# The even layer's 31-tap depthwise convolution computed on TensorE instead of VectorE and GpSimd, with two score banks in the attention beside it

## The chip, the cores and the metric

The kernel runs on one core of one Trainium2 chip. The metric is the device time of one execution in microseconds (us); everything is float32. Engines are called PE (TensorE), DVE (VectorE), ACT (ScalarE), POOL (GpSimd) and SP (SyncE, which only issues transfers).

## The reference, cut to what matters

The program chains three networks over 256 tokens of width 1024. The change lies in the second one, in its even layer. There, one half of the layer is an attention of 8 heads over 512 keys (256 context keys and 256 own keys), and the other half is a gated convolution over the tokens:

```
glu  = a * sigmoid(b)                       # 512 channels, from one projection of the normed tokens
conv = sum over tap 0..30 of  w[tap, channel] * glu[token + tap - 15, channel]  + bias[channel]
y    = silu(layer_norm(conv) * g + b)       # mean and variance over the 512 channels of a token
x    = x + gate * (concat(attention, y) @ w_out)
```

Each channel is convolved by itself (depthwise). The layer is followed by a router and a mixture of 16 experts with 12 MB of weights each, the first of two such mixtures.

## The kernel before

Everything is written out by hand: each engine runs its own function (`even_pe`, `even_act`, `even_dve`, `even_pool`), whose order in the code is the engine's order, and engines wait for one another by named marks (`pe_s`, `act_s`, `dve_s`, `pool_s`). `claim` makes PE wait until a PSUM bank has been read out.

**Weights.** SP loads weight chunks of 2 MB in the order in which they are used, each into the next of 6 slots of `ring`. A chunk is loaded as soon as PE has used the chunk that stood 6 before it in that slot. Around the change the order is: the layer's projections with pieces of the conditioning matrix (`ada1_0` to `ada1_5`), then `ada1_6` to `ada1_11`, `ev_out0`, `ev_out1`, `memkv0`, and three parts (g1, u0, d0) of the first expert. So `ev_out0` waits for the use of `ada1_6`, and d0 for the use of `ada1_11`. The part g0 of the first expert goes into `spare` and `p_buf` after the last transposition of the attention (`b2.T15`), the next ones wait for the use of `ev_out0` and `ev_out1`, and u1 and d1 for the router's logits.

**The attention `b2`.** 16 units (a head's 128 queries by 512 keys) run through a software pipeline of 19 steps. In step i, PE computes the scores of units i and i+1 if i is even (L713), transposes the exponentials of unit i-2 (L738) and multiplies those of unit i-3 with the values (L747). DVE takes a unit's row minimum, ACT the exponential, the copy of the transposed exponentials and the output. The list `scores` names the banks for scores: with `THREE = (4, 3, 2)` the scores of unit i wait for the exponential of unit i-3, with `TWO = (4, 2)` for that of unit i-2.

**Beside the attention**, after each step, a hook `also` runs on each engine. On PE (`beside_b2`) it multiplies with one piece of the conditioning matrix in each of steps 0 to 5 (`ada_rows_pe`, 8 matmuls of a 128x32 stationary tile by 512 columns, one after another for the four column groups of the array, L950), turns the result into columns in step 8 (L962, L965), and does the layer norm's sums with matmuls in steps `LN_AT` = 9, 12 and 15 (L1410, L1416, L1422).

**The convolution.** Channels lie on partitions, four tiles of 128, tokens along the row, with 15 zeros on either side in `glu`. DVE does tile 1 before the attention and tiles 2 and 3 partly before it and partly in its hook in steps 0 to 8 (`conv31`, one instruction per tap and tile, L1487); POOL does tile 0 (`conv31_pool`, two instructions per tap, L1645 and L1647). The PE sum of step 9 waits for both.

Of the kernel before, what the change touches and what calls it, by code (L numbers as in the profile page):

```python
# [22 lines left out]
S = 256  # L23
# [61 lines left out]
def onehots():  # L85
# [11 lines left out]
    for i in range(512):  # L97
# [8 lines left out]
        ("mem_norm_3", 16), ("ev_conv_w_2", 124), ("ev_conv_b_2", 4), ("ev_ln_g_2", 4), ("ev_ln_b_2", 4),  # L106
# [22 lines left out]
def expert_order(a):  # L129

    return a.reshape(-1, 2, P, 4).transpose(0, 1, 3, 2).reshape(-1, P)


def columns(name, a):

    a = np.asarray(a)
    if name == "norm2_g_2":
        return expert_order(a)
    if name == "ada_b_2":
        b = a.reshape(2, 6, D)  # L140
        return np.concatenate([expert_order(b[l, v]) if v in (3, 4) else b[l, v].reshape(-1, P) for l in range(2) for v in range(6)])
    return a.reshape(-1, P)
# [145 lines left out]
def program(nc, A, out, planned):  # L288
# [12 lines left out]
    with ctx:  # L301
# [1017 lines left out]
        glu = view(10752, 4, S + 30)  # L1319
        cv = view(11896, 4, S)  # L1320
        catT = view(12920, 8, S)
# [51 lines left out]
        ADA_COLUMNS = 8  # L1373
        TAPS_FIRST, TAPS_BEFORE = 5, 8

        def even_pe():
# [19 lines left out]
            def beside_b2(step):  # L1396
                if step < 12 - ADA_FIRST:
                    ada_rows_pe(12 + ADA_FIRST + step)
                elif step == ADA_COLUMNS:
                    ada_columns_pe(1)  # L1400
                layer_norm_sums(step)

            def layer_norm_sums(step):


                if step == LN_AT:
                    claim(LN_BANK)
                    waits(t_, (pool_s, "conv0"), (dve_s, "conv3"))
                    for k in range(4):
                        ins = t_.matmul(bank[LN_BANK][:, 0:S], ones128, cv[:, k, :], start=(k == 0), stop=(k == 3))  # L1410
                    ins.then_inc(*pe_s.signals("ln0"))
                elif step == LN_AT + 3:
                    waits(t_, (act_s, "cv sq"))
                    for t in range(2):
                        for k in range(4):
                            ins = t_.matmul(bank[LN_BANK][:, t:t + 1], cv_sq[:, k, P * t:P * t + P], constant("one"), start=(k == 0), stop=(k == 3),  # L1416
                                            skip_group_check=True)
                    ins.then_inc(*pe_s.signals("ln1"))
                elif step == LN_AT + 6:
                    waits(t_, (pool_s, "ln.rstd"))  # L1420
                    for t in range(2):
                        ins = t_.matmul(bank[LN_BANK][:, P * t:P * t + P], stats[:, 64 + t:65 + t].to_broadcast([P, P]), ident, start=True, stop=True,  # L1422
                                        skip_group_check=True)
                    ins.then_inc(*pe_s.signals("ln2"))

            attention_pe("b2", units2, before=turned("kx", kx_items) + turned("qx", qx_items), also=beside_b2)
# [6 lines left out]
        def even_act():  # L1433
# [7 lines left out]
            for t in range(2):  # L1441
                a.activation(view(12920, 2, D)[:, t, :], mem_raw[0][:, t, :], ACT.Square, accum_out=stats[:, 104 + t:105 + t])\
                    .then_inc(*act_s.signals(*(["nmem.ss"] if t else [])))
            for i in range(2):
                a.wait_ge(*pe_s.after(f"ev_glu{i}.acc1"))
                a.activation(pT_buf[:, i, :], bank[acc_banks(f"ev_glu{i}") + 1][:, :], ACT.Sigmoid).then_inc(*act_s.signals(f"ev_glu{i}.free1"))
            for t in range(2):
# [16 lines left out]
            attention_act("b2", units2, before=[(dve_s, "glu1")], also=beside_b2)  # L1464
# [6 lines left out]
        LN_AT = 9  # L1471
        LN_BANK = 5
        TAPS_AT = [TAPS_BEFORE + n for n in (0, 3, 6, 9, 12, 15, 18, 20, 22, 23)]

        def conv31(taps, tiles):

            v = nc.vector
            for tap in taps:
                for k in tiles:
                    w = col("ev_conv_w_2", 4 * tap + k)  # L1480
                    src = glu[:, k, tap:tap + S]
                    if tap == taps[0]:
                        v.wait_ge(*dve_s.latest())
                    else:
                        v.wait_ge(dve_s.sem, dve_s.n - (len(tiles) - 1))
                    if tap:
                        ins = v.scalar_tensor_tensor(out=cv[:, k, :], in0=src, scalar=w, in1=cv[:, k, :], op0=ALU.mult, op1=ALU.add)  # L1487
                    else:
                        ins = v.tensor_scalar(cv[:, k, :], src, w, col("ev_conv_b_2", k), ALU.mult, ALU.add)
                    ins.then_inc(*dve_s.signals(*([f"conv{k}"] if tap == CONF_K - 1 else [])))  # L1490
# [57 lines left out]
        def even_dve():  # L1548
# [14 lines left out]
            for i in range(2):  # L1563
# [4 lines left out]
                if i == 0:  # L1568
                    conv31(range(CONF_K), [1])
            conv31(range(TAPS_FIRST), [2, 3])  # L1570
            rope_raw_dve(0)
            conv31(range(TAPS_FIRST, TAPS_BEFORE), [2, 3])
# [8 lines left out]
            def conv_and_norm(step):  # L1581
                if step == ADA_COLUMNS + 1:
                    ada_columns_dve(1)
                if step < LN_AT:
                    conv31(range(TAPS_AT[step], TAPS_AT[step + 1]), [2, 3])
                elif step == LN_AT + 1:
                    v.wait_ge(*pe_s.after("ln0"))
                    v.tensor_scalar(mean, bank[LN_BANK][:, 0:S], 1.0 / 512, None, ALU.mult).then_inc(*dve_s.signals("ln0"))
                    v.wait_ge(*pool_s.after("conv0"))
# [5 lines left out]
                elif step == LN_AT + 3:  # L1595
# [5 lines left out]
            attention_dve("b2", units2, also=conv_and_norm)  # L1601
# [5 lines left out]
        def context_pool():  # L1607

            waits(nc.gpsimd, (pe_s, "ada.e0"), (dve_s, "y.e3"), (dve_s, "branch_a0.free1"))
# [8 lines left out]
        def even_pool():  # L1618
# [6 lines left out]
            g.wait_ge(*dve_s.after("glu0"))  # L1625
            g.wait_ge(*pe_s.after("hx.T3"))
            conv31_pool(range(0, 15))
            for t in range(2):
                rstd_pool("ev_q_g", *[b[:, 8 * t:8 * t + 8] for b in q_ss], HD, tile=t)
                if t == 0:  # L1630
                    conv31_pool(range(15, 18))
            conv31_pool(range(18, CONF_K))
            head_norm_pool("ln", 1, width=512)

        def conv31_pool(taps):

            g = nc.gpsimd
            tmp = [flat_xn[:, 1024 + 256 * i:1280 + 256 * i] for i in range(2)]
            for tap in taps:
                w = col("ev_conv_w_2", 4 * tap)  # L1640
                src = glu[:, 0, tap:tap + S]
                if tap:
                    if tap >= 3:
                        g.wait_ge(pool_s.sem, pool_s.n - 1)
                    g.tensor_scalar(tmp[tap % 2], src, w, None, ALU.mult).then_inc(*pool_s.signals())  # L1645
                    g.wait_ge(*pool_s.latest())
                    g.tensor_tensor(cv[:, 0, :], cv[:, 0, :], tmp[tap % 2], ALU.add)\  # L1647
                        .then_inc(*pool_s.signals(*(["conv0"] if tap == CONF_K - 1 else [])))
                else:
                    g.tensor_scalar(cv[:, 0, :], src, w, col("ev_conv_b_2", 0), ALU.mult, ALU.add).then_inc(*pool_s.signals())  # L1650

# [1414 lines left out]
```

## Time and profile before

| | us |
|---|---|
| median of 3 runs | 2328.44 (2328.24 to 2328.85) |
| the profiled execution | 2325.14 |
| its span in the trace | 2322.9 |
| PE busy | 1960.7 (84%) |
| DVE busy | 594.2 (26%) |
| ACT busy | 290.4 (13%) |
| POOL busy | 131.7 (6%) |
| chain that ended last: PE, DMA, DVE | 64%, 32%, 2% |

Busy shares are averages over stages with different limits, so the stage that is changed has to be read from the trace by itself. Times in the trace count from the span's start. The attention `b2` runs from 416 to 476 us, the first mixture of experts from about 536 us.

### The profile page before, as it was taken

Reading aid. Unit: us, or ns where it says so; the run is one execution under the profiler, and the core shown is the slowest. Engines: PE = TensorE matmul, PEld = TensorE weight load, DVE = VectorE, ACT = ScalarE, POOL = GpSimd, SP = SyncE. Lnnn points to the kernel's source line nnn. Section 1 sums busy time; section 2 is a strip of 40 time slices with the busy share of each in tenths; the row PEclk is TensorE's granted clock in tenths of the full one; section 3 lists DMA queues with packets and bytes.
Section 4 is the critical chain, followed back from the end, with each engine's and each line's share of the span. In section 5 each row is a group of like instructions: output and inputs, shape, how many; then the busy total and the mean of one; then the engine's idle time right before and its main releaser. Section 6 shows DMA issues by size and latency. Waiting matters only on the chain.

```text
span 2322.9 us, 30376 instructions
## 1 busy us (share of the span) xinstructions
PE 1960.7 (84%) x12649; PEld 1153.0 (50%) x12649; DVE 594.2 (26%) x1686; ACT 290.4 (13%) x750; POOL 131.7 (6%) x177
## 2 busy tenths in 40 slices
PE   8999999899655566699966556669999999999999
PEld 4455556555322222387532223224568854548874
DVE  1323337712000000122210000004625411334430
ACT  1023411431000000010200000001500001300000
POOL 0200006400000000000000000002100000010000
PEclk9999999899888887899997887879999999999999
DMA  9658347839999999975899999999234444324420
GB/s 365 250 187 318 128 163 256 324 116 382 425 426 427 427 426 427 388 228 217 333 425 426 426 427 425 427 422 336 73 110 145 155 147 151 109 73 146 163 107 18
DMA packets 191439, 634.48 MB, mean 273 GB/s; under 512 B 6529, under 2 KB 90641, under 8 KB 158840
## 3 DMA queue, kind: packets, MB, share of 16 engines
q1 hardware_dynamic: 186912, 623.79, 69.2%
q0 software_dynamic: 1504, 5.83, 0.7%
q10 hardware_dynamic: 2936, 3.66, 0.4%
q8 instruction: 61, 1.00, 0.2%
q14 instruction: 26, 0.21, 0.0%
HBM read 632.15 MB, written 1.09 MB: 273 GB/s over the span
## 4 chain that ended last, share of the span: by engine, by line
PE 64%; DMA 32%; DVE 2%; ACT 1%; issue 1%; POOL 0%; SPq 0%; DVEq 0%; ACTq 0%
DMA ring<-in_moe_w_down 32%; PE bank L647 17%; PE bank L662 17%; PE bank L2573 7%; PE bank L2050 4%; PE bank L999 3%; PE bank L747 2%; PE bank L713 1%; PE bank L950 1%; PE bank L738 1%; PE bank L2225 1%; PE bank L2034 1%; PE bank L1952 1%; PE bank L2529 1%; DVE arena L1487 1%; PE bank L561 1%
## 5 line engine op out<-in xcount | busy, mean ns | idle before, releaser
L2034 PE MATMUL bank<-ring,arena 128*32 128x256 f32 x3968 | 303.0, 461 | 185.9 <-DMA ring<-in_moe_w_up 113.2
L2034 PEld LDWEIGHTS bank<-ring,arena 128*32 128x32 f32 x3968 | 138.8, 128 | 336.6 <-DMA ring<-in_moe_w_up 147.3
L647 PE MATMUL bank<-ring,hT 128*128 128x512 f32 (+2 forms) x704 | 299.1, 583 | 5.0 <-DVE hT L2213 2.9
L662 PE MATMUL bank<-xn,ring 128*128 128x256 f32 x1280 | 276.6, 379 | 0.0
L662 PEld LDWEIGHTS bank<-xn,ring 128*128 128x128 f32 x1280 | 243.2, 190 | 33.0
L2050 PE MATMUL bank<-ring,arena 128*32 128x256 f32 x1984 | 162.7, 485 | 76.9 <-DMA ring<-in_moe_w_down 66.9
L647 PEld LDWEIGHTS bank<-ring,hT 128*128 128x128 f32 x704 | 133.6, 192 | 157.3 <-issue 153.8
L2573 PE MATMUL bank<-ring,arena 128*128 128x512 f32 x352 | 151.6, 592 | 0.0
L2050 PEld LDWEIGHTS bank<-ring,arena 128*32 128x32 f32 x1984 | 73.2, 134 | 154.5 <-DMA ring<-in_moe_w_down 83.4
L1843 DVE TENSOR_TENSOR arena<-arena,bank 128x256 f32<-128x256 f32 x32 | 13.5, 421 | 495.2 <-ACT arena L1904 495.2
L662 PE MATMUL bank<-hT,ring 128*128 128x256 f32 x512 | 111.3, 379 | 1.3 <-ACT arena L1357 1.3
L1904 ACT ACTIVATE arena<-bank 128x256 f32<-128x256 f32 x32 | 12.3, 383 | 769.6 <-PE bank L2034 769.6
L2573 PEld LDWEIGHTS bank<-ring,arena 128*128 128x128 f32 x352 | 66.8, 190 | 82.8 <-issue 82.3
L662 PEld LDWEIGHTS bank<-hT,ring 128*128 128x128 f32 x512 | 97.0, 190 | 15.4 <-issue 2.3
L1846 DVE TENSOR_TENSOR arena<-bank,arena 128x256 f32<-128x256 f32 x32 | 13.6, 424 | 249.4 <-PE bank L2050 249.4
L2623 DVE SCALAR_TENSOR_TENSOR arena<-arena,cols 128x256 f32<-128x256 f32 x176 | 71.5, 477 | 0.0
L2611 DVE TENSOR_TENSOR arena<-bank,arena 128x512 f32<-128x512 f32 x44 | 30.4, 691 | 152.6 <-PE bank L662 140.9
L999 PE MATMUL bank<-ring,hT 128*128 128x512 f32 x128 | 69.0, 631 | 0.4 <-ACT arena L1009 0.4
L510 POOL TENSOR_SCALAR stats<-stats 128x1 f32<-128x1 f32 (+7 forms) x34 | 7.6, 223 | 1082.8 <-DVE stats L410 450.6
L647 PE MATMUL bank<-ring,arena 128*128 128x512 f32 (+1 forms) x160 | 64.8, 562 | 2.9 <-ACT arena L579 2.9
L747 PE MATMUL bank<-arena,pT_buf 128*128 128x64 f32 (+1 forms) x408 | 62.6, 278 | 0.6 <-ACT pT_buf L770 0.3
L747 PEld LDWEIGHTS bank<-arena,pT_buf 128*128 128x128 f32 x408 | 56.8, 201 | 6.9 <-ACT pT_buf L770 2.6
(409 smaller groups left out, 1837.8 us busy)
## 6 DMA issues: line engine op xcount, KB each, us to landing
ring<-in_moe_w_gate SPq DMA_DIRECT2D x62, 2048.0 KB, 26.5
ring<-in_moe_w_up SPq DMA_DIRECT2D x62, 2048.0 KB, 26.0
ring<-in_moe_w_down SPq DMA_DIRECT2D x62, 2048.0 KB, 26.1
ring<-in_ada_w SPq DMA_DIRECT2D x24, 2048.0 KB, 11.7
ring<-in_w_up SPq DMA_DIRECT2D x44, 1024.0 KB, 7.6
ring<-in_w_in SPq DMA_DIRECT2D x11, 2048.0 KB, 17.5
ring<-in_w_down SPq DMA_DIRECT2D x10, 2048.0 KB, 7.8
ring<-in_w_out SPq DMA_DIRECT2D x6, 2048.0 KB, 22.3
```

The source lines that it names most:

```text
L561: ins = nc.tensor.transpose(bank[b][0:n, at:at + tokens], src(t), constant("ident", tokens)[:, 0:tokens])
L647: ins = t_.matmul(bank[b][:, 0:n], lhsT(k)[:, P * t:P * t + P], w[:, k, c0:c0 + n], start=(k == 0), stop=(k == kt - 1))
L662: ins = t_.matmul(bank[b][:, 256 * (j % 2):256 * (j % 2) + 256], w[:, k, P * j:P * j + P], rhs[:, k, :], start=(k == 0), stop=(k == 7), sk ...
L713: t_.matmul(score_bank(i, scores)[:, 0:u["keys"]], u["q"], u["k"], start=True, stop=True)\
L738: ins = t_.transpose(bank[6 + j % 2][0:n, P * k:P * k + P], p[:, P * k:P * k + n], ident)
L747: ins = t_.matmul(bank[j % 2][:, 0:v.shape[-1]], pT_buf[0:n, j % 2, P * k:P * k + P], v, start=(k == 0), stop=(k == len(u["v"]) - 1))
L999: ins = t_.matmul(bank[GM_BANK][:, :], hT[:, k, P * t:P * t + P], slot(name)[:, k, :], start=(k == 0), stop=(k == 7))
L2034: ins = t_.matmul(bank[4][32 * j:32 * j + 32, at:at + 256], xs_now[b][:, 4 * (c % 2) + k, :], w(k)[:, 256 * j:256 * j + 256], start=(c % 2 ...
L2050: ins = t_.matmul(bank[6][32 * j:32 * j + 32, 0:256], hidT[b][:, f % 2, 32 * (f // 2):32 * (f // 2) + 32], w(k)[:, 256 * j:256 * j + 256], ...
L2573: ins = t_.matmul(bank[b][:, :], actT[:, f, P * t:P * t + P], w[:, k, 512 * half:512 * half + 512], start=(f == 0), stop=(f == FF_TILES - 1))
L2611: v.tensor_tensor(up_buf[i % 2][:, 2 * t:2 * t + 2, 2:2 + S], bank[acc_banks(name) + t][:, :].rearrange("p (k s) -> p k s", s=S), by_token ...
L2623: ins = v.scalar_tensor_tensor(out=dst, in0=src, scalar=w, in1=dst, op0=ALU.mult, op1=ALU.add)
```

## The change

Each channel tile k is now convolved by 32 matmuls on PE. The 128 channels are taken in four quarters q of 32. For each quarter, the 128 partitions of a matmul's input hold the quarter's 32 channels four times, and copy j is shifted by j tokens (`shifted[k]`). The stationary tile (128x32) is four diagonal blocks with the weights of taps 4g to 4g+3, so that one matmul adds four taps; 8 groups g cover 32 taps (the last has weight zero). The four quarters write the four column groups of one bank. The parts:

- POOL builds the stationary tiles by multiplying the constant `fold` with the tap weights (`tap_weights_pool`): tiles 0 to 2 early, before its load of the context, into `spare`, tile 3 after the hx turn into `xn`.
- The shifted copies are transfers from SBUF to SBUF: 16 of them for tiles 0 and 1 together, issued by ACT between the two sigmoids of the gate, and 16 each for tiles 2 and 3, issued by POOL after the norm of the queries (`shift_pool`).
- PE runs the matmuls in halves of 16 in steps 0, 1, 2, 3, 5, 6, 7 and 8 of `b2` (`conv31_pe`). Four of the six conditioning pieces move from steps 0 to 5 to steps 9 to 13: they now stand in steps 4, 9, 10, 11, 12, 13. The columns move from step 8 to 16, the layer norm's sums from 9, 12, 15 to 10, 13, 16 and to bank 3.
- DVE only adds the bias while copying two tiles out of the bank, in steps 4 and 9 (`conv31_dve`). All its taps and those of POOL are gone.
- The attention uses `TWO` score banks, since bank 3 holds the convolution.

```diff
-        ADA_COLUMNS = 8
-        TAPS_FIRST, TAPS_BEFORE = 5, 8
+        ADA_BESIDE = (4, 9, 10, 11, 12, 13)
+        ADA_COLUMNS = 16
+        CONV_AT = {0: (0, 0), 1: (0, 1), 2: (1, 0), 3: (1, 1), 5: (2, 0), 6: (2, 1), 7: (3, 0), 8: (3, 1)}
...
+            def conv31_pe(k, half):
+                if half == 0:
+                    if k % 2 == 0:
+                        claim(CONV_BANK)
+                    t_.wait_ge(s_shift[max(0, k - 1)], 16 * 16)
+                    waits(t_, (pool_s, f"tap weights{k}"))
+                for g in range(4 * half, 4 * half + 4):
+                    for q in range(4):
+                        ins = t_.matmul(bank[CONV_BANK][32 * q:32 * q + 32, S * (k % 2):S * (k % 2) + S], tap_w[k][:, q, g, :],
+                                        shifted[k][:, q, 4 * g:4 * g + S], start=(g == 0), stop=(g == 7), skip_group_check=True)
...
-            attention_pe("b2", units2, before=turned("kx", kx_items) + turned("qx", qx_items), also=beside_b2)
+            attention_pe("b2", units2, before=turned("kx", kx_items) + turned("qx", qx_items), also=beside_b2, scores=TWO)
...
+                if i == 0:
+                    waits(a, (act_s, "nmem.ss"), (dve_s, "glu0"))
+                    for j, q in itertools.product(range(4), range(4)):
+                        a.dma_start(shifted01[32 * j:32 * j + 32, :, q, 0:SHIFTED], glu[32 * q:32 * q + 32, 0:2, j:j + SHIFTED]).then_inc(s_shift[0], 16)
...
-        LN_AT = 9
-        LN_BANK = 5
+        LN_AT = 10
+        LN_BANK = CONV_BANK
...
-                if i == 0:
-                    conv31(range(CONF_K), [1])
-            conv31(range(TAPS_FIRST), [2, 3])
...
+                if step in (4, 9):
+                    conv31_dve(step == 9)
...
+            tap_weights_pool(range(3))
...
+            tap_weights_pool([3])
...
-            conv31_pool(range(18, CONF_K))
+            waits(g, (dve_s, "glu1"), (pe_s, "ev_q.acc1"))
+            shift_pool(2)
+            waits(g, (pe_s, "hm0.T3"))
+            shift_pool(3)
```

PE, the first steps of `b2` before (L713 scores, L738 transpositions, L747 values, L950 conditioning):

```order
L713 MATMUL bank<-arena 128x512 x2
L950 MATMUL bank<-ring,arena 32x512 x16
L713 MATMUL bank<-arena 128x512 x2
L738 MATMUL bank<-const,p_buf 128x128 x4
L950 MATMUL bank<-ring,arena 32x512 x8
L738 MATMUL bank<-const,p_buf 128x128 x4
L747 MATMUL bank<-arena,pT_buf 128x64 x4
L950 MATMUL bank<-ring,arena 32x512 x8
```

One conditioning piece (8 matmuls) stands in each step, two of them together in the second row.

The same place in the changed kernel, where the lines are L716, L741, L750 and L953, and L1441 is the convolution:

```order
L716 MATMUL bank<-arena 128x512 x2
L1441 MATMUL bank<-arena,spare 32x256 x32
L716 MATMUL bank<-arena 128x512 x2
L741 MATMUL bank<-const,p_buf 128x128 x4
L1441 MATMUL bank<-arena,spare 32x256 x16
L741 MATMUL bank<-const,p_buf 128x128 x4
L750 MATMUL bank<-arena,pT_buf 128x64 x4
L1441 MATMUL bank<-arena,spare 32x256 x16
L716 MATMUL bank<-arena 128x512 x2
L741 MATMUL bank<-const,s_buf 128x128 x4
L750 MATMUL bank<-arena,pT_buf 128x64 x4
L953 MATMUL bank<-ring,arena 32x512 x8
```

The convolution stands where the conditioning stood, and only one conditioning piece is left among the first nine steps.

PE in the changed kernel from step 12 to the end of step 16 (L953 conditioning, L1421 the sums of squares, L965 and L968 the columns, L1427 the last matmuls of the layer norm; the repeated column rows are cut off):

```order
L953 MATMUL bank<-ring,arena 32x512 x8
L1421 MATMUL bank<-const,xn 128x1 x8
L716 MATMUL bank<-arena 128x512 x2
L741 MATMUL bank<-const,p_buf 128x128 x4
L750 MATMUL bank<-arena,pT_buf 128x64 x4
L741 MATMUL bank<-const,p_buf 128x128 x4
L750 MATMUL bank<-arena,pT_buf 128x64 x4
L741 MATMUL bank<-const,s_buf 128x128 x4
L750 MATMUL bank<-arena,pT_buf 128x64 x4
L965 MATMUL bank<-const,arena 128x24
L968 MATMUL bank<-const,arena 64x8 x2
```

Before, these columns stood in step 8; now they stand two steps from the end.

POOL in the changed kernel, from the norm of the memory tokens to the layer norm:

```order
L1662 TENSOR_TENSOR xn<-const,cols 128x256 x4
L513 TENSOR_SCALAR stats<-stats 128x8
L516 TENSOR_TENSOR stats<-stats,const 128x8
L513 TENSOR_SCALAR stats<-stats 128x8
L516 TENSOR_TENSOR stats<-stats,const 128x8
L1670 DMA hT<-arena 32x284 x16
L1670 DMA arena<-arena 32x284 x16
L513 TENSOR_SCALAR stats<-stats 128x2
L516 TENSOR_TENSOR stats<-stats,const 128x2
```

Between the queries' norm and the layer norm, where POOL had its taps 18 to 30, it now issues 32 transfers.

## Rows read from the trace of the kernel before

**Rows 1.** Chain that ended last: start us, us, what; 329 to 620 us.
```profile
369.46 3.57 PE bank L950 x32
...
414.09 1.08 PE bank L561 x8
...
416.26 1.15 PE bank L713 x4
...
458.05 0.59 PE bank L738 x4
458.64 0.84 PE bank L747 x8
...
463.24 1.81 PE bank L1416 x16
...
474.00 1.80 PE bank L747 x16
...
535.96 7.09 PE bank L2034 x128
...
563.44 26.17 DMA ring<-in_moe_w_down
```

**Rows 2.** Windows: start:end, length, busy (instructions) of PE, PEld, DVE, ACT, POOL; granted clock, DMA share, GB/s.
```profile
416.26:475.80 59.54, 55.87 (x372) 37.68 (x372) 39.35 (x89) 25.36 (x65) 19.98 (x25) 0.86 0.67 257
420.00:440.00 20.00, 18.03 (x140) 8.58 (x132) 19.64 (x39) 6.25 (x17) 14.35 (x16) 1.00 1.06 393
440.00:445.00 5.00, 3.32 (x16) 1.92 (x16) 4.93 (x13) 2.65 (x8) 0.00 (x0) 0.75 1.03 440
445.00:450.00 5.00, 5.00 (x28) 4.40 (x26) 4.13 (x11) 2.63 (x7) 0.00 (x0) 0.50 0.96 401
465.00:470.00 5.00, 5.00 (x27) 3.43 (x26) 1.58 (x5) 1.99 (x6) 2.06 (x4) 0.66 0.04 13
475.80:480.20 4.40, 1.10 (x8) 0.87 (x9) 0.76 (x2) 4.20 (x8) 0.00 (x0) 0.98 0.90 363
```

**Rows 3.** Groups of PE instructions, 416.2 to 475.9 us: count, busy us, mean ns, idle before.
```profile
L713 PE MATMUL bank<-arena 64*128 64x512 f32 x32 | 10.9, 761 | 4.1 <-ACT p_buf L779 2.6 <-DVE arena L587 1.1 <-ACT s_buf L779 0.4
```

**Rows 4.** The same view of DVE, 365 to 480 us.
```profile
L1487 DVE SCALAR_TENSOR_TENSOR arena<-arena,cols 128x256 f32<-128x256 f32 x90 | 52.2, 614 | 1.8
```

**Rows 5.** Timeline of ACT: start us, us, engine, line, operation [idle before].
```profile
1.72 0.64 ACTq L1051 DMA_DIRECT2D p_buf<-in_onehots  x1
...
31.38 0.34 ACTq L1070 DMA_DIRECT2D bias_rows<-s_buf  x1
...
387.07 0.60 ACT L1446 ACTIVATE pT_buf<-bank 128x512 f32<-128x512 f32 x1 [16.98 <-PE bank L662]
```

**Rows 6.** Timeline of POOL.
```profile
283.76 0.91 POOL L1610 DMA_DIRECT2D arena<-in_ctx  x1 [166.84 <-DVE arena L1194]
...
372.85 0.83 POOL L1647 TENSOR_TENSOR arena<-arena,xn 128x256 f32<-128x256 f32 x1
...
408.83 1.84 POOL L513 TENSOR_TENSOR stats<-stats,const 128x8 f32<-128x8 f32 x1
...
1592.39 0.54 POOL L2682 DMA_DIRECT2D small<-in_gla_gate_w  x1
...
1687.49 0.99 POOL L2689 DMA_DIRECT2D arena<-in_w_in_gla  x1 [2.11 <-DVE arena L2666]
```

**Rows 7.** Transfers, 395 to 480 us: target, queue, count, KB each, median us to landing.
```profile
small<-in_moe_w_r POOLq DMA_DIRECT2D x1, 64.0 KB, 2.2
```

**Rows 8.** Timeline of SP's transfers.
```profile
435.88 0.38 SPq L2956 DMA_DIRECT2D ring<-in_moe_w_down  x1
...
474.03 0.33 SPq L2938 DMA_DIRECT2D spare<-in_moe_w_gate  x1
```

## What the change should do

> **What bounds the kernel now.** I read the chain that ended last first, between 329 and 620 us. It runs over PE up to 563 us and from there over the expert weights [rows 1]. From 563 us the mixture is paced by the transfers, and how early their stream starts is set by PE: part g0 is issued at 474.03, after the attention's last transposition, and later parts wait for the output projection and the router. So what `b2` gains or loses should arrive at the end unchanged, as long as the weights before it land in time.
>
> Then I cut out `b2`, from its first scores at 416.26 to the end of the last product at 474.00 + 1.80 = 475.80, as one window [rows 1, 2]. Its length is 59.54 us, PE is busy for 55.87, at a mean granted clock of 0.86. The reader should see two regimes. From 420 to 440 DVE is busy for 19.64 of 20 us while PE has gaps; the gaps before scores are 4.1 us in all, mostly for ACT, which itself is behind DVE's taps [rows 2, 3]. After that DVE falls idle and PE is busy all the time, but at a clock of 0.75 and then 0.50 (the lower level, 1.2 instead of 2.4 GHz). So DVE bounds the first third, and PE the rest.
>
> **What PE has to do.** A mean clock of 0.86 says that 0.14 x 59.54 = 8.3 us of the window were lost to the lower level. PE's own work at full clock is then 55.87 - 8.3 = 47.6 us; the other 3.7 us are gaps. 47.6 + 8.3 + 3.7 = 59.6 closes.
>
> **The change part by part.**
>
> *Removed.* 90 of DVE's tap instructions in the trace, 52.2 us busy [rows 4], and all of POOL's. Those before 416 us are worth nothing: PE goes from work to work, and `b2` starts when the queries are turned (414.09 and 1.08 us, then their copy), which comes after ACT's copies, not after taps [rows 1]. Those within `b2` are worth at most the 3.7 us of gaps, plus what the lower clock costs after those gaps.
>
> *Added on PE.* 4 tiles x 32 = 128 matmuls of a 128x32 stationary tile by 256 columns over four column groups. The first expert's gate and up products have just this form: 128 records, that is 64 matmuls, in 7.09 us at full clock [rows 1]. So the convolution costs 2 x 7.09 = 14.2 us. I see no price below this; the conditioning's form gives the same rate (16 matmuls of 512 columns in 3.57 us, 0.22 each, half of it per 256 columns), and it stands between pieces of the attention already.
>
> PE then has 47.6 + 14.2 = 61.8 us of work at full clock. That is above today's 59.5 us even before any gap. The work removed from DVE bought at most 12 us (3.7 gaps + 8.3 clock), and the convolution costs more than that.
>
> *Moved on PE.* Conditioning pieces, columns and layer norm cost the same wherever they stand, except by the clock. The sums of squares are 16 records of one column in 1.81 us [rows 1], and after them the clock was 0.66 in the window from 465 to 470, some 3.4 us at the lower level, a cost of 1.7 us [rows 2]. They now stand in step 13, behind a conditioning piece, which is denser. The columns (8 and 24 wide) move to step 16, two steps from the end, after two steps that hold attention alone. I take one such stretch of low clock in the changed kernel, 1.7 us; the bounds are none (0) and both with the tail of the attention (3.4).
>
> *Two score banks.* The scores of an even step now wait for the exponential of the unit just before, which ACT finishes in the odd step ahead. After its transposition in that step PE still has a product (0.84 us) and, in steps 1 to 13, a piece of convolution or conditioning (1.8 us each: half of 3.57) [rows 1]; ACT needs a copy and an exponential over 512 columns, which at the 0.60 us of its gate over 512 columns [rows 5] are some 1.3 us. So PE comes later than ACT. Only in steps 14 to 16, where ACT also copies the conditioning sums out, do I count 0.3 us. Bounds: 0, and the same 4.1 us that scores wait today [rows 3].
>
> *DVE* has two biased copies of 128x512 in place of the taps, about 0.7 us each, behind which the next row minimum waits; PE is not waiting for DVE by then. I count nothing.
>
> *ACT* issues 16 transfers after the first gate. Its issues take 0.34 to 0.64 us, 5 to 10 us in all, and it waits 16.98 us for PE there [rows 5]. Hidden; they land 25 us before they are needed.
>
> *POOL, tap weights.* 12 operations of 128x256 early, at some 0.83 us each 10 us, in an idle time of 166.84 us ahead of the context's load [rows 6]; the 4 for tile 3 take 3.3 us in POOL's idle time before the taps of today. Hidden.
>
> *POOL, shifts.* This is the part that can hurt. POOL is done with the queries' norm at 408.83 + 1.84 = 410.7, a little earlier without taps, and then issues 32 transfers one after another. Its issues take 0.54 to 0.99 us; the shortest is the one with the fewest rows (16), the longest the one with the most (1024 short runs) [rows 6]. These have 32 rows, so I take 0.6: tile 2 is issued by 420.3, tile 3 by 429.9, and landed 2.2 us later [rows 7]. PE needs tile 2 in step 5 and tile 3 in step 7. Step 7 comes after four pairs of scores (1.1 each), six transpositions and five products (0.59 or less, and 0.84), six half tiles and one conditioning piece (1.8 each): about 24 us after 416.3, at 440. There are 8 us to spare. With 0.99 each the last lands at 444.6, 4 to 5 us late.
>
> The Trainium skill (DMA: Bandwidth & Descriptors, "Anatomy of one DMA") gives a transfer issued by GpSimd about 2.0 us of fixed cost from setup to completion; the 2.2 us of the trace agree, and the rule changes nothing so long as issues follow each other without waiting for landings.
>
> *SP.* With the conditioning pieces used later, `ev_out1` to d0 are issued in steps 9 to 13 instead of 1 to 5 (the last at 435.88 today [rows 8]). In the new order, with step 7 at 440 and some 4 us a step, that is 448 to 464 us. Five chunks of 2.1 MB at some 400 GB/s [rows 2] take 26 us, so d0 lands near 473, and g0 is behind it as today. The output projection needs `ev_out1` only 15 us later, and the experts start at 536. Nothing is late. The cover is some 20 us for the projection and 60 for d0.
>
> **Sum.** 61.8 (work) + 1.7 (clock) + 0.3 (banks) = 63.8 us. The mean clock is rounded, by up to 0.3 us in this sum; I take 63.6, against 59.5: +4.1 us. The profiled execution would go from 2325.1 to 2329.2, and the median of the runs, 3.3 us above it, from 2328.44 to 2332.5. A difference of 0.2% (4.66 us) is about what a measurement of this kernel can tell from no change, so this lies just inside "no change", at 0.18%.
>
> **A rule weighed.** In the trace PE is busy for 5.00 of 5.00 us at a clock of 0.50 between 445 and 450, so being busy alone doesn't bring the clock back; what ended it was the layer norm's sums over 256 columns. The Trainium skill (TensorE: Matmul & The Clock Gate, "What's actually happening") says that the gate opens with how busy PE has recently been. Taken plainly, a stage without gaps would then hold 2.4 GHz throughout. By the trace I lose 1.7 us, by the rule nothing; the rule is the second case below.
>
> **The rivals.**
>
> 1. *The forecast*, one stretch of low clock and no late copy: 2332.5. Chance 0.45.
> 2. *Full clock throughout*: 61.8 + 0.3, +2.5 us: 2330.9. For it: no gaps are left. Against it: one-column matmuls and columns remain. Chance 0.17.
> 3. *The shifts come late*, the case on the slower side. POOL's issues serialize behind something, each taking 0.99 us or more. From 0.86 us on (32 x 0.86 + 2.2 + 410.7 = 440.4) step 7 waits, and each further 0.1 us costs 3.2 us. At 1.1 us it waits 7.7 us, and a gap of that size brings the clock down for another 1.7: +4.1 + 9.4 = 13.5 us, 2341.9. At 0.99, with the clock, it is about 2338. Against it: the rows of 0.54 and 0.64. Chance 0.17.
> 4. *PE falls behind its own sum*: two banks leave gaps as wide as today's (3.7 us) and both low-clock stretches come (another 1.7): +9.5, 2337.9. Chance 0.13.
> 5. *Faster*: this needs the attention's transpositions and products to shrink when a dense piece stands before them. The 32 pieces (a transposition of 0.59 us or a product of 0.84 each [rows 1]) would have to lose 0.2 us each, since 61.8 must fall below 54.8. Weight loads are busy 37.68 of 59.54 us, so something can hide, but in steps with conditioning today the transposition is not shorter. At the decision point 2323.7. Chance 0.08.
>
> **The numbers.** Slower by over 0.2%: rivals 3 and 4, 0.30, and 0.12 of the forecast's own spread, which ends at the boundary: 0.42. Faster: 0.08. Same: 0.50. The range goes from 2328.0 (full clock, some weight loads hidden) to 2341.0 (late shifts).
>
> **What would show it.** In the window of `b2`: a length near 63.6 us, PE busy in nearly all of it, the convolution at 14.2 us and a clock of 0.94 to 1.00; DVE busy for less than 20 us of it. Before step 7 no wait for a transfer. g0 is issued 4 us later than 474.03, and the mixture starts and ends 4 us later. I am wrong if the convolution's matmuls take other than 0.11 us each, if a wait of PE for the shift stands in step 5 or 7, if the clock stays low with PE full, or if the mixture's stream doesn't move with the end of `b2`.

## The result

| | before | changed |
|---|---|---|
| median, us (lowest to highest), 12 runs each | 2326.99 (2323.29 to 2331.93) | 2333.78 (2329.03 to 2342.36) |
| ratio, 95% interval | | 1.0034 [1.0024, 1.0044] |
| profiled execution, span, us | 2325.14, 2322.9 | 2329.93, 2328.1 |
| `b2`, first scores to end of the last product, us | 59.54 | 65.24 |

The changed kernel is slower by 0.34%, 5.6 to 10.2 us by the interval; the medians differ by 6.8 us. The forecast was +4.1 us or 0.18%, just inside the 0.2% that it took for "no change". The measured difference lies beyond that, in a case to which it gave 0.42. The sign and the place were right, the size was too small.

The changed kernel's page, engines' busy time in us and share:

```profile
PE 1966.6 (84%) x12905; PEld 1155.3 (50%) x12905; DVE 546.8 (23%) x1595; ACT 290.1 (12%) x750; POOL 100.9 (4%) x164
```

The changed kernel's chain that ended last (start us, us, what), around `b2`:

```profile
413.63 0.77 DVE arena L590 x2
414.39 0.30 issue
414.69 1.13 PE bank L716 x4
415.82 3.59 PE bank L1441 x64
...
420.47 0.59 PE bank L741 x4
421.06 1.86 PE bank L1441 x32
...
453.46 1.92 PE bank L1415 x8
455.38 0.44 PE bank L741 x4
...
466.13 1.88 PE bank L1421 x16
...
473.49 0.34 PE bank L968 x4
473.83 0.33 PE bank L965 x2
...
476.92 3.02 PE bank L750 x16
...
484.36 22.33 PE bank L650 x48
...
567.49 26.28 DMA ring<-in_moe_w_down
```

From 414.69 us on the chain runs over PE alone: no tap and no row minimum of DVE is left on it. The output projection starts at 484.36 instead of 480.22, and the mixture's piece of the chain, the transfer of 26 us, at 567.49 instead of 563.44 [rows 1]. What `b2` gained arrived at the end.

Windows of the changed kernel (columns as in [rows 2]): `b2` as a whole, then cut where the clock falls.

```profile
414.69:479.94 65.25, 65.24 (x628) 41.61 (x628) 16.35 (x45) 24.74 (x65) 10.37 (x22) 0.98 0.79 282
414.69:477.20 62.51, 62.51 (x617) 39.07 (x617) 15.06 (x37) 24.07 (x64) 10.15 (x22) 1.00 0.79 282
477.20:479.94 2.74, 2.73 (x14) 2.54 (x12) 1.28 (x9) 0.67 (x2) 0.22 (x1) 0.50 0.88 278
```

PE is busy for 65.24 of 65.25 us. For 62.5 us it has the full clock, and the last 2.74 us run at the lower level. Against [rows 2] the stage lost its 3.7 us of gaps and most of its low clock, and gained more PE work than that.

The groups of PE in the changed kernel, 414.6 to 485 us, columns as in [rows 3]:

```profile
L716 PE MATMUL bank<-arena 64*128 64x512 f32 x32 | 9.0, 640 | 1.1 <-DVE arena L590 1.1
```

The scores wait once, for the queries' copy before the first of them. The waits for ACT of [rows 3] are gone, in spite of two banks.

Timeline of POOL in the changed kernel, the norm of the queries and its 32 transfers:

```profile
405.59 1.69 POOL L516 TENSOR_TENSOR stats<-stats,const 128x8 f32<-128x8 f32 x1
407.23 7.96 POOL L1670 DMA_DIRECT2D hT<-arena  x16
415.18 7.83 POOL L1670 DMA_DIRECT2D arena<-arena  x16
```

The last issue ends at 423.0, and these transfers land 5.6 to 5.9 us (median) after their issue. Step 7 needs them at 439.6 and finds them there.

### The profile page after: what moved, and what is told of

It reads as the page before. It is cut to its first block, busy times and chain, and to the rows that moved or that the text cites. A ratio compares the mean times of both kernels' runs of the same rounds, so it can differ in the third digit from the quotient of the medians.

```text
span 2328.1 us, 30805 instructions
## 1 busy us (share of the span) xinstructions
PE 1966.6 (84%) x12905; PEld 1155.3 (50%) x12905; DVE 546.8 (23%) x1595; ACT 290.1 (12%) x750; POOL 100.9 (4%) x164
## 4 chain that ended last, share of the span: by engine, by line
PE 65%; DMA 32%; DVE 1%; ACT 1%; issue 1%; POOL 0%; SPq 0%; DVEq 0%; ACTq 0%
DMA ring<-in_moe_w_down 32%; PE bank L665 17%; PE bank L650 17%; PE bank L2590 6%; PE bank L2067 4%; PE bank L1002 3%; PE bank L750 2%; PE bank L953 2%; PE bank L716 2%; PE bank L741 1%; PE bank L2242 1%; PE bank L2051 1%; PE bank L1969 1%; PE bank L2546 1%; PE bank L564 1%; PE bank L1441 1%
## 5 line engine op out<-in xcount | busy, mean ns | idle before, releaser
L750 PE MATMUL bank<-arena,pT_buf 128*128 128x64 f32 (+1 forms) x408 | 62.9, 279 | 0.4 <-ACT pT_buf L773 0.3
L773 ACT ACTIVATE pT_buf<-bank 128x256 f32<-128x256 f32 (+3 forms) x120 | 43.6, 363 | 133.2 <-PE bank L741 133.0
L750 PEld LDWEIGHTS bank<-arena,pT_buf 128*128 128x128 f32 x408 | 56.8, 201 | 6.4 <-ACT p_buf L782 2.0
```

What stands on the lines that cost most here:

```text
L750: ins = t_.matmul(bank[j % 2][:, 0:v.shape[-1]], pT_buf[0:n, j % 2, P * k:P * k + P], v, start=(k == 0), stop=(k == len(u["v"]) - 1))
L773: a.activation(pT_buf[0:n, j % 2, 0:kt * P], bank[6 + j % 2][0:n, 0:kt * P], ACT.Copy)\
```

## The experiments

Three batches of kernels, each against the kernel before on its own chip (2328.43; 2326.58 over 23 runs; 2327.71 over 23 runs). "Stage" is `b2` as above. For a single run no ratio is given.

### What the convolution on PE costs

**A quarter of it** (changed kernel; groups 0 and 7 of the 8 alone, so 24 of the 32 taps are left out):

```diff
-                for g in range(4 * half, 4 * half + 4):
+                for g in ([7] if half else [0]):
```

> The changed kernel with 8 of the 32 convolution matmuls per tile (groups 0 and 7 of 8); the convolution is therefore incomplete, everything else is unchanged. Theory A (the attention stage is now nothing but PE's work, 65.25 us): 24 of 32 matmuls less are 11.1 us less work, so the stage from first scores to last product falls to 54 us plus whatever gaps open, 54 to 57 us, and the mixture starts 8 to 11 us earlier. Rival B (the transfers of the shifted copies or the two score banks hold the stage): the stage falls by under 4 us, with waits in place of the matmuls.

**Twice** (changed kernel; each matmul of the convolution is issued twice, so most taps count double):

```diff
-                for g in range(4 * half, 4 * half + 4):
+                for g in [g for g in range(4 * half, 4 * half + 4) for _ in range(2)]:
```

> The changed kernel with each convolution matmul issued twice (so the sums come out double where they accumulate). Theory A: 14.75 us more PE work, so the stage grows from 65.25 to 80 us and the whole by 14.75 us (profiled execution near 2344.7). Rival B (PE has hidden slack): less than 10 us.

The stage as a window, first with a quarter:

```profile
416.54:472.94 56.40, 55.75 (x436) 34.66 (x436) 16.56 (x45) 24.68 (x65) 9.65 (x20) 0.96 0.89 316
```

and with the double:

```profile
415.79:495.33 79.54, 79.53 (x884) 48.90 (x884) 16.36 (x45) 24.75 (x65) 9.50 (x20) 0.98 0.63 223
```

The double adds 14.3 us to the stage (79.54 - 65.24) and 16 us to the execution (2345.97 us). The quarter takes 8.8 us off; three quarters of 14.75 would be 11.1, but 0.65 us of gaps and a lower mean clock came back (0.96). Its execution took 2323.43 us. In both traces the clock is at its lower level at the first scores (2.10 and 2.08 us instead of 1.13), and it had fallen ahead of them, before the edited lines run; more on this under "The rest of the size". So the stage is PE's work and nothing that the convolution could hide behind: nearly every microsecond added is paid.

### Two banks and moved pieces, without the convolution

**Two banks alone** (kernel before; all three engines):

```diff
-            attention_pe("b2", units2, before=turned("kx", kx_items) + turned("qx", qx_items), also=beside_b2)
+            attention_pe("b2", units2, before=turned("kx", kx_items) + turned("qx", qx_items), also=beside_b2, scores=TWO)
```

> The kernel before with only the score banks cut from three to two. Theory A: DVE's taps bound the first half of the stage and PE waits there anyway, so the stage stays within 1 us of 59.54 us. Rival C (two banks are a cost of their own in the changed kernel): 3 us or more longer, with longer waits of the scores for the exponentials.

**Two banks and the pieces moved** as in the change, taps still on DVE and POOL:

```diff
-        ADA_COLUMNS = 8
+        ADA_BESIDE = (4, 9, 10, 11, 12, 13)
+        ADA_COLUMNS = 16
...
-        LN_AT = 9
-        LN_BANK = 5
+        LN_AT = 10
+        LN_BANK = 3
```

> The kernel before with two banks and with the conditioning pieces, columns and layer norm in the steps of the changed kernel, the taps still on DVE and POOL. Theory A: the first nine steps stay at DVE's pace with PE emptier (five conditioning pieces, 9.3 us, move behind them), so the stage grows by 6 to 9 us to 66 to 69 us, and the clock is low for longer. Rival D (the moved pieces cost nothing, only the convolution does): within 2 us of 59.54.

With two banks alone the stage takes 63.90 us, 4.4 more than before. The group of the scores there:

```profile
L713 PE MATMUL bank<-arena 64*128 64x512 f32 x32 | 10.9, 761 | 7.5 <-ACT p_buf L779 5.1 <-ACT s_buf L779 1.3 <-DVE arena L587 1.1
```

The wait for ACT's exponentials goes from 3.0 [rows 3] to 6.4 us; the forecast that the stage stays within a microsecond was wrong. Of the 4.4 us, 2.7 are gaps. The other 1.6 are pieces of PE at the lower clock, and not all of them come from the banks: in this trace, too, the clock was low at the first scores (2.10 instead of 1.15 us). With the pieces moved as well, the stage as a window:

```profile
418.84:491.75 72.91, 61.55 (x372) 42.83 (x372) 39.40 (x89) 25.54 (x65) 19.93 (x25) 0.75 0.58 216
```

13.4 us longer than before, also more than expected: 11.4 us of gaps, and a mean clock of 0.75. The execution took 2342.88 us. The same layout in the changed kernel has no gap. The layout is thus bad with empty steps and DVE's taps, and good with the convolution in the steps and the taps gone; this run does not say which of the two differences does it.

### An earlier place for the columns

Changed kernel, pieces in steps 4 to 9 and the columns in step 11, so that the columns are followed by more work:

```diff
-        ADA_BESIDE = (4, 9, 10, 11, 12, 13)
-        ADA_COLUMNS = 16
+        ADA_BESIDE = (4, 5, 6, 7, 8, 9)
+        ADA_COLUMNS = 11
...
-                elif step == ADA_COLUMNS + 2:
+                elif step == ADA_COLUMNS + 4:
```

> The changed kernel with the conditioning pieces in steps 4 to 9 and the columns in step 11 instead of 16. Theory A says that PE's work is the same, and that the columns and sums near the end brought the low clock from 477 to 487 us, worth 1.3 us in the stage and 1.5 us of the output projection: the stage falls from 65.25 to about 64 us if the low clock goes, and the kernel gains 1 to 3 us over the changed one, still slower than before by 2 to 5 us. Rival: the low clock only moves to step 13, and nothing is gained.

Measured: 2339.03 us (6 runs), 1.0052 [1.0037, 1.0066] of before, where a gain of 1 to 3 us over the changed kernel was expected. The interval overlaps with the changed kernel's, so that the timing alone does not tell the two apart; the stages do (72.29 us busy against 65.24). Windows of that kernel after the pieces are used up:

```profile
465.00:470.00 5.00, 5.00 (x27) 4.19 (x28) 1.78 (x8) 1.85 (x5) 0.00 (x0) 0.65 0.35 144
470.00:475.00 5.00, 5.00 (x25) 4.99 (x24) 0.00 (x0) 2.14 (x5) 0.00 (x0) 0.50 0.00 0
475.00:480.00 5.00, 5.00 (x20) 3.49 (x20) 1.97 (x9) 1.44 (x4) 1.66 (x3) 0.50 0.00 2
```

PE is busy for every microsecond, with attention, the layer norm's sums and columns, and the clock is at its lower level for about 20 us. In the changed kernel the conditioning pieces of steps 9 to 13 stand among this work, and the clock is 1.00 to 477.2 us. So the late place of pieces and columns, which the prediction costed as neutral but for one stretch of 1.7 us, was worth 7 us of stage (72.29 against 65.24), or 4 against the longer of the changed kernel's two traces (68.67, below).

### What the taps cost on DVE and POOL

Here a new theory was tested: that the removed work was slow only because DVE and POOL did it at the same time.

**All four tiles on DVE** (kernel before, three banks, POOL has no taps):

```diff
-        TAPS_FIRST, TAPS_BEFORE = 5, 8
+        TAPS_FIRST, TAPS_BEFORE = 4, 7
...
-                    conv31(range(CONF_K), [1])
+                    conv31(range(17), [0, 1])
+            conv31(range(17, CONF_K), [0, 1])
...
-            conv31_pool(range(0, 15))
...
```

All of POOL's taps are left out, and each step's share of DVE's taps is set anew.

> The kernel before with all four tiles' taps on DVE and none on POOL or PE. In the trace of before a tap takes 0.66 us while POOL works and about 0.45 us after it has stopped. Theory A (DVE's pace sets the first half of the attention stage, and POOL's taps slow DVE's): 124 taps at 0.47 us are 58 us, 33 us of room before the stage, 25 us in nine steps, so the stage is within 2 us of 59.5 us although DVE does a third more taps. Rival: a tap takes 0.6 us without POOL too, and the stage grows by 8 us or more.

**The same, measured again** beside the changed kernel:

> The same kernel as with all four tiles on DVE, timed again for a narrower interval: 0.996 to 0.998 of before, with an attention stage of 50 to 52 us.

> The changed kernel again, on the same chip as the run above. Theory A: the stage is PE's work and always 65 to 67 us whatever the low clock does elsewhere; the kernel is 0.3% slower than before, and 0.6% (14 us) slower than the one with all taps on DVE, which is what the two stages differ by (65.2 - 50.2 = 15).

**POOL's taps taken away** (kernel before; DVE's taps as they were; tile 0 is left out and filled with zeros):

```diff
-            conv31_pool(range(0, 15))
+            g.memset(cv[:, 0, :], 0.0).then_inc(*pool_s.signals("conv0"))
...
-                if t == 0:
-                    conv31_pool(range(15, 18))
-            conv31_pool(range(18, CONF_K))
```

> The kernel before without POOL's taps: tile 0 of the convolution is left out (filled with zeros), DVE has exactly the taps of before. Theory E (POOL's taps and DVE's taps slow each other, so that a DVE tap takes 0.61 us on average instead of 0.48): the steps 0 to 4 of the attention stage fall from some 4.2 us to PE's pace of 3.7, the gaps of PE and with them the low clock go, and the stage falls from 59.54 us to 50 to 52 us, as with all four tiles on DVE. Rival (the stage got short in that experiment for another reason): the tap stays near 0.6 us and the stage within 2 us of 59.5.

| kernel | median, us (runs) | ratio to before | stage, us | PE busy | clock |
|---|---|---|---|---|---|
| all on DVE | 2319.84 (10) | 0.9970 [0.9960, 0.9980] | 50.19 | 50.08 | 0.97 |
| all on DVE, again | 2321.44 (11) | 0.9983 [0.9973, 0.9993] | 50.23 | 50.13 | 0.97 |
| changed, again | 2335.65 (12) | 1.0033 [1.0021, 1.0045] | 68.67 | 68.66 | 0.92 |
| POOL's taps away | 2317.87 (1) | | 49.88 | 49.87 | 0.97 |

DVE's taps in the trace of the kernel before, within the stage (416 to 441 us), beside the row minimum, which reads from PSUM:

```profile
L1487 DVE SCALAR_TENSOR_TENSOR arena<-arena,cols 128x256 f32<-128x256 f32 x34 | 19.3, 619 | 0.4
L810 DVE TENSOR_REDUCE row_min<-bank 128x1 f32<-128x512 f32 x6 | 4.1, 681 | 1.4 <-PE bank L713 1.4
```

The same without POOL's taps:

```profile
L1487 DVE SCALAR_TENSOR_TENSOR arena<-arena,cols 128x256 f32<-128x256 f32 x36 | 15.3, 482 | 0.4
L810 DVE TENSOR_REDUCE row_min<-bank 128x1 f32<-128x512 f32 x7 | 4.8, 686 | 1.4 <-PE bank L713 1.4
```

Nothing was changed on DVE, yet a tap takes 482 instead of 619 ns; the row minimum takes the same. The 619 is itself a mean over two stretches. POOL's last tap operation ends at 435.0 us, and the trace of the kernel before, from 416 to 435 and from 436 to 447 us, has

```profile
L1487 DVE SCALAR_TENSOR_TENSOR arena<-arena,cols 128x256 f32<-128x256 f32 x24 | 15.0, 676 | 0.3
L1487 DVE SCALAR_TENSOR_TENSOR arena<-arena,cols 128x256 f32<-128x256 f32 x20 | 8.6, 481 | 0.3
```

So a tap costs 676 ns beside POOL and 481 once POOL is quiet, in one and the same execution. Six taps and a row minimum fill a pipeline step, so 0.8 us a step by the means and 1.2 us while POOL works, and without POOL's taps PE no longer falls behind. The Trainium skill (SBUF — State Buffer, "SBUF: two separate sides") says that VectorE and GpSimd share a pair of ports, which an operation of DVE with two SBUF inputs must have for itself against a GpSimd operation that reads SBUF. The trace agrees on which instruction is slowed: the tap, with two inputs in SBUF, is, and the row minimum, with one in PSUM, is not. That POOL's taps slow DVE's is shown by the run without them; that the ports are the way in which they do it is the page's account, and beyond this agreement no run here tests it.

With all 120 of its taps on DVE the group reads:

```profile
L1487 DVE SCALAR_TENSOR_TENSOR arena<-arena,cols 128x256 f32<-128x256 f32 x120 | 49.6, 481 | 0.8
```

DVE does 120 taps in less time (49.6 us) than 90 beside POOL (52.2 [rows 4]). POOL's taps, 60 operations in that stretch, were worth less than nothing. The second measurement, 0.9983, lies just above the 0.996 to 0.998 expected of it. The stage falls to 50.2 us, 15 us below the changed kernel's; it had been expected within 2 us of 59.5, so the theory was right on the tap and far too cautious on what it is worth. Of its 9.3 us against before, 2.3 to 2.7 were given back ahead of it: it starts at 418.93 and 418.57 instead of 416.26, in both traces with a mean clock of 0.91 between 200 and 240 us, where before has 0.96 and the changed kernel 1.00. The code of PE is the same there; I have no cause for it.

**All on DVE, but with two banks:**

> All four tiles on DVE, with two score banks instead of three. With three banks the stage took 50.19 us. Theory A: two banks cost only where the exponential of the unit just before is held up behind DVE's taps, and DVE is now nearly at PE's pace in the steps, so the scores of even steps wait a little: 51 to 54 us. Rival C (two banks cost 4 us wherever they stand): 54 us or more.

The stage takes 61.82 us instead of 50.19, with PE busy for 58.34 at a clock of 0.83: 3.5 us of gaps for ACT's exponentials and the rest low clock. The execution took 2326.64 us. My theory gave this at most 54 us and missed. But not all of the 11.6 us are the banks' price. The stage's first 5 us here, and with three banks:

```profile
415.87:421.00 5.13, 5.13 (x24) 1.34 (x28) 2.99 (x7) 0.78 (x2) 0.00 (x0) 0.58 1.05 388
418.93:424.00 5.07, 5.07 (x38) 1.54 (x40) 3.85 (x8) 0.78 (x2) 0.00 (x0) 1.00 1.06 388
```

The clock of 0.58 stands for some 2 us (0.42 x 5.13, an estimate), and it had fallen before the first scores, where the two kernels do not differ.

**One tile on PE in its gaps ahead of `b2`, three on DVE, three banks:**

```diff
-                    conv31(range(CONF_K), [1])
+                    conv31(range(CONF_K), [0])
...
+            conv31_pe(0)
             turn_pe("qx", qx_items, before=[(dve_s, "rope q")])
+            conv31_pe(1).then_inc(*pe_s.signals("conv1"))
```

> Tile 1 on PE, in the gaps before the attention where PE waits for ACT (half before and half behind the turn of the queries), tiles 0, 2 and 3 on DVE, none on POOL; three score banks and the pieces in the steps of before. Theory A: DVE's share inside the stage falls to 17 taps of two tiles (16 us in nine steps), below PE's pace, and PE has 49 to 50 us of work without the convolution: the stage starts 1 us later and takes 51 to 54 us, so the kernel is 4 to 7 us faster than before. Rival: the gaps before the stage don't hold the matmuls and DVE stays the pace: within 1 us of before.

PE's two halves of that tile in this kernel's chain:

```profile
414.80 1.86 PE bank L1409 x32
416.67 1.02 PE bank L564 x8
417.69 1.86 PE bank L1409 x32
```

Measured: 2322.59 us (12 runs), 0.9980 [0.9971, 0.9989]; stage 51.52 us. DVE's taps take 483 ns here too. It is better than before, because POOL's taps are gone, and no better than the kernel with nothing on PE: the gaps it fills cost about 1 us more ahead of the stage.

## Why the prediction was right or wrong

**What bounds the stage: right as far as it went.** PE at its own work with no gaps, and the shift passed on one to one (+4.14 us at the output projection, +4.05 at the mixture). The 4.14 are the stage's 5.70 less 1.57 by which the stage starts earlier. It starts earlier because before has a stretch of low clock near 221 us that this execution of the changed kernel lacks; PE's code is the same there. So it is luck that the later pieces moved by just the 4.1 us of the forecast, and that the profiled execution took 2329.93 us where 2329.2 was forecast.

**The term that was mis-sized most: "PE's own work at full clock is 47.6".** It subtracted 0.14 x 59.54 = 8.3 us as lost to the lower clock, as if every piece took twice as long there. The chain shows otherwise. Before, at the lower level:

```profile
443.44 2.08 PE bank L713 x4
445.52 1.04 PE bank L738 x4
446.57 1.60 PE bank L747 x8
...
448.87 0.55 PE bank L962 x2
449.42 0.34 PE bank L965 x4
...
454.19 2.80 PE bank L1410 x8
```

and the same pieces at full clock, where POOL's taps were away:

```profile
442.32 1.06 PE bank L713 x4
443.38 0.59 PE bank L738 x4
443.97 0.84 PE bank L747 x8
...
445.00 0.34 PE bank L965 x4
445.34 0.33 PE bank L962 x2
...
448.79 1.78 PE bank L1410 x8
```

Scores go from 2.08 to 1.06, but the columns' 8-wide matmuls take 0.34 at either level, the 24-wide 0.55 and 0.33, a transposition 1.04 and 0.59. Added up piece by piece over before's slow pieces, the low clock cost 7.0 us, not 8.3. Part of the difference are the 8-wide matmuls, and part is time in which the clock was low while PE had nothing to do, as before the scores at 443.44, and which costs nothing. PE's own work at full clock was thus 55.87 - 7.0 = 48.9 us, 1.3 more than the prediction had. In the changed kernel it still cost 1.3: the last 2.74 us at half clock, mostly the last product (3.02 instead of 1.80). The clock gave back 5.7 us where 8.3 - 1.7 = 6.6 were counted.

**The convolution: 14.75 us, not 14.2.** 3.59 + 6 x 1.86. The expert's products, from which the rate was read, take 7.09 us for 128 records, 1.77 for 32. Each of the six pieces that stand alone takes 0.09 more than that, and the two in a row at the start together 0.05 more.

**Gaps: right.** 3.7 us gone, and none came. (The 4.1 us of [rows 3] that served as a bound hold 1.1 us ahead of the first scores, outside the stage.)

**Two banks: right here, for a reason that was only half seen.** They open no gap in the changed kernel. In the two kernels of before's layout, with DVE's taps and steps of attention alone, the stage grew by 4.4 and 11.6 us, of which gaps are 2.7 and 3.4 and the rest is clock, not all of it theirs. The prediction covered them with 1.8 us of other work in each odd step. That this work is needed is not shown. With a quarter of the convolution each step has under 0.5 us of it, and the scores of that kernel read

```profile
L716 PE MATMUL bank<-arena 64*128 64x512 f32 x32 | 10.0, 699 | 1.8 <-DVE arena L590 1.1 <-ACT p_buf L782 0.5
```

that is, 0.7 us of waits beside those for the queries. What this kernel shares with the changed one, and not with the two that lost, is a DVE without taps in front of its row minima. Which of the two counts for more was not tested.

The sum again, in measured terms: +14.75 (convolution) - 3.66 (gaps) - 5.7 (clock) + a rest of 0.3 = +5.7, which is 65.24 - 59.54. The rest has about the size of what the layer norm's sums (1.92 and 1.88 instead of 1.78 and 1.81) and the columns take longer where they now stand.

**DVE, ACT, POOL, SP: right.** Within the stage none of them is on the chain that ended last. A transfer's issue takes 0.49 us on POOL and 0.67 on ACT, against 0.6 and 0.3 to 0.6; ACT's 16 are hidden in its wait for PE. POOL's land 5.6 to 5.9 us after their issue, where 2.2 was taken; the shorter issues made up for it. d0 is issued at 466.20 and lands 13.7 us later, near 480, where 473 was forecast, still well before the experts start at 540; g0 is issued at 476.95, 2.9 us later instead of 4. The late shifts (rival 3) did not happen: from the last landing near 429 to step 7 at 439.6 there are over 10 us.

**The full clock throughout (rival 2) did not happen either.** In the changed kernel the clock fell at 477.2 us, 11 us after the last conditioning piece and after the columns. The kernel with the earlier columns, above, has PE busy for 5.00 of 5.00 us and a clock of 0.50 in two windows on end. The Trainium skill (TensorE: Matmul & The Clock Gate, "What's actually happening") has the gate open with how busy PE has been; by these two windows PE can be busy without a gap, as the trace counts it, and stay at 1.2 GHz, and the measurement decides.

**The rest of the size.** The second trace of the changed kernel, windows of its stage before and after the clock falls near the end:

```profile
415.91:478.20 62.29, 62.29 (x598) 37.33 (x598) 14.39 (x36) 23.87 (x63) 9.28 (x19) 0.97 0.75 269
478.20:484.58 6.38, 6.37 (x34) 6.09 (x32) 1.96 (x9) 0.91 (x2) 0.39 (x1) 0.50 0.70 234
```

That is 68.67 us, 3.4 more than the first, with the same instructions. 2 us of it stand at the start, where the chain has the scores at 2.08 instead of 1.13 and the first piece of the convolution slowed as well:

```profile
415.91 2.08 PE bank L716 x4
417.98 4.63 PE bank L1441 x64
```

The stage is then 5.7 or 9.1 us longer than before's, and the output projection starts 4.1 or 8.8 us later (484.36 or 489.01 against 480.22). The timed 5.6 to 10.2 us would fit a mixture of the two, but before has only one trace here, so that is not shown. I had expected 65 to 67 us whatever the clock does elsewhere, and that missed. I forecast from one execution and gave the clock at the stage's start no term; how often either form comes isn't settled by two traces.

The other runs say more of the low clock at the start. Of the thirteen traces of all kernels, six have a mean clock of 1.00 between 200 and 240 us. In five of these (all but the first trace of the changed kernel) the clock falls at some 413 us, ahead of the first scores, with a mean of 0.57 to 0.61 from 412 to 420 us. The seven others have 0.91 or 0.96 between 200 and 240 us, and 1.00 from 412 to 420. Both sorts hold kernels with and without the change, so this is no effect of the convolution: an execution loses a few microseconds in one place or in the other (by the share of the clock some 1.6 to 3.6 us in the one, 3.1 to 3.4 in the other, estimates from these means). The first trace of the changed kernel lost them in neither and is the favourable case. The stage lengths of single traces here carry an uncertainty of 2 to 3 us.

**What the prediction did not ask.** It took the removed taps as worth at most 12 us, and that was right: the stage without POOL's taps is 9.7 us shorter. But it saw only PE as the way to get them. The 614 ns of [rows 4] for a tap of DVE were taken as they stood, though they mix 676 ns beside POOL with 481 after it, and both could be read in the trace of before. The work bought for 14.75 us of PE time was to be had for nothing. Against the kernel with all taps on DVE, run on the same chip, the changed one is 14.2 us slower (2335.65 against 2321.44), 0.6%. Their stages differ by 18.4 us (68.67 against 50.23), 14.75 of it the convolution's own, and 2.7 are given back because the other stage starts later.

**Left open.** Why the mean clock between 200 and 240 us is 0.91 in some traces and 1.00 in others whose code on PE is the same there, and how that goes with the low clock at 413 us. How often the changed kernel's stage has 65 or 69 us. Two score banks with all taps on DVE and work moved into their empty steps was not tried.

## What to carry to other kernels

Before moving work to the engine that bounds a stage, ask whether the engine that has it now is slow by itself or because of a neighbour: compare the mean duration of one instruction where both are busy with a stretch where one is alone, and not the mean over both. A gain that consists of removed gaps and clock is limited by what both cost, and must be larger than the full price of the added work. Low clock is not to be costed as share times length, since 8-wide matmuls took 0.34 us at either level and a gap costs nothing at either; take each piece from a row at either level. A buffer taken away (three banks to two) opened no gap in one layout and some 3 us of gaps in two others, so test it in the layout it will have. Where two traces of one kernel differ by 3 us in a stage, a difference of that size between two kernels needs more than one trace of each.

## What the runs showed of the hardware that was not expected

- A DVE tap of 128x256 (two inputs in SBUF) takes 481 to 483 ns alone and 676 beside POOL's element operations (416 to 435 us); a reduction of 128x512 out of PSUM takes 681 to 686 either way.
- PE's granted clock stays at 0.50 with PE busy for 5.00 of 5.00 us, from 470 to 480 us in the kernel with the columns in step 11; from 461.8 us on PE had attention pieces, one-column sums and columns of 8 and 24 there. In the changed kernel, with conditioning pieces among the same kind of work, it was 1.00 until 11 us after the last of them.
- Four transpositions take 0.59 us behind a column-group piece or scores, and 0.44 behind a product or a sum. A column-group piece of 32 records takes 1.86 us between other pieces, and two in a row take 3.59.
- Transfers from SBUF to SBUF of 35.5 KB are issued by POOL in 0.49 us each and land 5.6 to 5.9 us later, beside a load at some 320 to 380 GB/s; the small load from memory of [rows 7] took 2.2.
